# A folded MLP's third pair of up tiles, its copies and squares, its low parts and its even turns put in another order

## The reference, cut to what matters

```
def mlp_sq_relu(hn, w_up, w_down):
    return jnp.square(jax.nn.relu(hn @ w_up)) @ w_down

h = h + mlp_sq_relu(rmsnorm(h, norm_mlp[i]), w_up[i], w_down[i])    # w_up 1024 x 4096, w_down 4096 x 1024
```

## Time and profile before

| what | us |
|---|---|
| median of 3 runs | 2661.4 (2658.84 to 2661.52) |
| profiled execution | 2656.41 |
| its span, first to last instruction | 2654.7 |
| PE matmuls busy | 2531.4 (95% of the span) |
| DVE busy | 1892.3 (71%) |
| ACT busy | 1143.5 (43%) |
| POOL busy | 802.0 (30%) |
| mean granted TensorE clock | 0.989 of full speed |

### The profile page before, as it was taken

One profiled execution on the slowest core, in us unless ns is written; L12 is line 12 of the kernel. 1 busy time (PEld: TensorE's weight loads), 2 busy tenths in 40 slices (PEclk: granted clock), 3 DMA queues, 4 the chain that ended last, 5 costly groups with the idle time before them and its releaser, 6 DMA issues.

```text
span 2654.7 us, 32483 instructions
## 1 busy us (share of the span) xinstructions
PE 2531.4 (95%) x11896; PEld 2081.2 (78%) x11896; DVE 1892.3 (71%) x2552; ACT 1143.5 (43%) x1860; POOL 802.0 (30%) x594
## 2 busy tenths in 40 slices
PE   7999999899999989998999999989999998999898
PEld 6788888787888768886778888878788876788677
DVE  7677655658666789998665657665766678999866
ACT  6555433535434444443442323353534344443344
POOL 2000000034232466664420000002423245666542
PEclk9999999999999999999999999999999999999999
DMA  3000100123333323321221001012233342323122
GB/s 134 29 25 25 32 25 24 56 71 107 104 118 120 123 96 116 107 96 56 88 95 40 25 32 40 24 47 97 80 115 108 115 133 104 109 95 124 52 64 80
DMA packets 78639, 207.63 MB, mean 78 GB/s; under 512 B 8672, under 2 KB 10736, under 8 KB 78496
## 3 DMA queue, kind: packets, MB, share of 16 engines
q1 hardware_dynamic: 75552, 195.85, 22.3%
q0 software_dynamic: 2224, 7.54, 0.8%
q10 hardware_dynamic: 720, 2.36, 0.2%
HBM read 163.25 MB, written 42.47 MB: 77 GB/s over the span
## 4 chain that ended last, share of the span: by engine, by line
PE 57%; issue 18%; DVE 15%; ACT 4%; POOL 3%; DMA 2%; DVEq 0%; ACTq 0%; POOLq 0%; SPq 0%
PE gemm_ps L732 8%; PE gemm_ps L734 8%; PE gemm_ps L733 8%; PE s_ps L732 7%; PE s_ps L733 6%; PE s_ps L734 6%; DVE wlo L2303 3%; PE to_ps L733 3%; PE to_ps L734 3%; PE to_ps L732 3%; DVE a_blocks L2390 2%; DMA hid_raw<-hidden 2%; DVE b_blocks_lo L2390 2%; POOL hid_raw L1244 2%; PE to_ps L838 1%
## 5 line engine op out<-in xcount | busy, mean ns | idle before, releaser
L732 PE MATMUL gemm_ps<-a_hi,whi 128*128 128x512 f32 x1024 | 424.4, 414 | 20.7 <-DVE a_lo L1914 10.7
L734 PE MATMUL gemm_ps<-a_hi,wlo 128*128 128x512 f32 x1024 | 402.5, 393 | 0.0
L733 PE MATMUL gemm_ps<-a_lo,whi 128*128 128x512 f32 x1024 | 401.5, 392 | 0.0
L732 PEld LDWEIGHTS gemm_ps<-a_hi,whi 128*128 128x128 f32 x1024 | 194.3, 190 | 61.1 <-issue 20.4
L2303 DVE TENSOR_TENSOR wlo<-wraw,whi 128x512 fp32r<-128x512 f32 (+1 forms) x204 | 213.9, 1049 | 33.3 <-ACT whi L1595 32.8
L1244 POOL TENSOR_TENSOR hid_raw<-hid_raw 128x512 f32<-128x512 f32 x120 | 197.0, 1650 | 103.2 <-DVE a_blocks L2390 42.3
L734 PEld LDWEIGHTS gemm_ps<-a_hi,wlo 128*128 128x128 f32 x1024 | 193.3, 189 | 42.8
L733 PEld LDWEIGHTS gemm_ps<-a_lo,whi 128*128 128x128 f32 x1024 | 194.4, 190 | 32.6 <-issue 1.4
L732 PE MATMUL s_ps<-a_blocks,whi 128*128 128x512 f32 x448 | 179.5, 401 | 31.4 <-DVE zt L2356 15.1
L2303 DVE TENSOR_TENSOR wlo<-wraw_a,whi 128x512 fp32r<-128x512 f32 (+1 forms) x204 | 175.6, 861 | 34.7 <-ACT whi L1595 33.7
L1595 ACT ACTIVATE whi<-wraw_a 128x512 fp32r<-128x512 f32 (+1 forms) x204 | 122.5, 602 | 168.5 <-PE s_ps L734 131.8
(11 more groups left out here) (392 smaller groups left out, 6347.0 us busy)
## 6 DMA issues: line engine op xcount, KB each, us to landing
wraw<-panels SPq DMA_DIRECT2D x90, 512.0 KB, 3.6
wraw<-folds SPq DMA_DIRECT2D x60, 512.0 KB, 4.3
wraw_a<-folds SPq DMA_DIRECT2D x60, 512.0 KB, 4.4
hid_raw<-hidden SPq DMA_DIRECT2D x120, 256.0 KB, 4.0
hidden<-sumsq SPq DMA_DIRECT2D x64, 256.0 KB, 3.5
hidden<-zs SPq DMA_DIRECT2D x32, 256.0 KB, 2.1
hidden<-zt SPq DMA_DIRECT2D x32, 256.0 KB, 2.0
h<-x_t SPq DMA_DIRECT2D x11, 512.0 KB, 5.4
```

The source lines that it names most:

```text
L732: nc.tensor.matmul(out, hi_w, hi_x, start=start, stop=False, skip_group_check=True)
L733: nc.tensor.matmul(out, hi_w, lo_x, start=False, stop=False, skip_group_check=True)
L734: return nc.tensor.matmul(out, lo_w, hi_x, start=False, stop=stop, skip_group_check=True)
```

## The change

- **Third pair sooner.** `RAMP` takes tile 2's parts in from (16, 3) to (17, 2) instead of (16, 5) to (17, 4). SP issues all four loads of tile 2 before the last stores of turn 15, and the loads of tile 3 before the raw weights of turn 19.
- **Copies ahead of squares.** In turn 16 ACT's squares of turn 15 move from blocks 0 and 1 to blocks 1 and 2, behind the copy of bank A.
- **Low parts.** `t3_lo` is gone; DVE makes block 4's low parts at (0, 0), and its others in turn 0 move to later blocks. The weights' low part at (0, 4) is made after the read of bank E.
- **Even turns.** At (n, 0) of turns 20, 22 up to 32, DVE's `w_ahead` moves behind `out_of(n, 0)`. GpSimd's S1 and S3 move from blocks 0 and 2 to blocks 2 and 4 in turns 20, 22 up to 30.

```diff
 RAMP = {...
-        (15, 6): [(0, 6), (1, 2)], (16, 0): [(1, 3)], (16, 1): [(1, 4)], (16, 2): [(1, 5)], (16, 3): [(1, 6)],
-        (16, 5): [(2, 0)], (16, 6): [(2, 1)], (17, 0): [(2, 2)], (17, 1): [(2, 3)],
-        (17, 2): [(2, 4)], (17, 3): [(2, 5)], (17, 4): [(2, 6)]}
+        (15, 6): [(0, 6), (1, 2)], (16, 0): [(1, 3)], (16, 1): [(1, 4)], (16, 2): [(1, 5)],
+        (16, 3): [(1, 6), (2, 0)], (16, 4): [(2, 1)], (16, 5): [(2, 2)], (16, 6): [(2, 3)],
+        (17, 0): [(2, 4)], (17, 1): [(2, 5)], (17, 2): [(2, 6)]}
+
+DEFERRED = [(0, 4)] + [(n, 0) for n in range(UPS + 4, TURNS, 2)]
...
-UP_LO = [x for x in UP_ORDER if x[0] != 4]
+UP_LO = UP_ORDER
...
                     elif n == 1:
-                        sp.wait_ge(up_t3_ready, 4 * layer + 3)
+                        sp.wait_ge(up_lo_ready, len(UP_LO) * layer + UP_LO.index((4, 2)) + 1)
...
                     store(n, B_RAW["B11"], C11, 1, c11_stored)
                     if n == UPS - 1:
-                        load_hidden(2, "B11")
+                        for name in ("B11", "B12", "B22", "B21"):
+                            load_hidden(2, name)
                     store(n, B_RAW["B22"], C22, 2, c22_stored)
-                load_hidden(2, "B12")
-                load_hidden(2, "B22")
                 store(UPS - 1, B_RAW["B12"], C12[(UPS - 1) % 2], 3, c12_stored[(UPS - 1) % 2])
-                load_hidden(2, "B21")
                 store(UPS - 1, B_RAW["B21"], C21, 4, c21_stored)
                 for n in range(UPS, TURNS):
                     s = n - UPS + 2
-                    if n + 2 < TURNS:
+                    if s != 3 and n + 2 < TURNS:
                         load_raw(n + 2)
                     if 2 < s < SUBS:
                         for name in ("B11", "B12", "B22", "B21"):
                             load_hidden(s, name)
+                    if s == 3:
+                        load_raw(n + 2)
...
-                def t3_lo(kk):
-                    gp.wait_ge(up_hi_ready, len(UP_ORDER) * layer + UP_ORDER.index((4, kk)) + 1)
-                    hi, lo = up_block(4, kk)
-                    nc.gpsimd.tensor_tensor(lo, late_part("T3", kk), hi, ALU.subtract).then_inc(up_t3_ready, 1)
...
-                for kk in range(4):
-                    t3_lo(kk)
                 for n in range(TURNS):
                     for j in range(BLOCKS):
                         if n == LAST - 2 and j == 0:
                             tail_adds(0)
-                        if n < LAST and j == 0:
+
+                        later = n >= UPS + 4 and n % 2 == 0 and n < LAST - 1
+                        if n < LAST and j == (2 if later else 0):
                             w_sum(n + 1, "S1")
-                        if n < LAST and j == 2:
+                        if n < LAST and j == (4 if later else 2):
                             w_sum(n + 1, "S3")
...
-                        if 1 <= n <= UPS and j == 0:
+                        if 1 <= n <= UPS and j == n // UPS:
                             square(n - 1, 2)
                             square(n - 1, 3)
-                        if 1 <= n <= UPS and j == 1:
+                        if 1 <= n <= UPS and j == 1 + n // UPS:
                             square(n - 1, 4)
...
                             if j == 1:
                                 t_part("T4", 3)
-                            for x in {1: late[0:2], 2: late[2:5], 3: late[5:8]}.get(j, ()):
+                            for x in late[0:4] if j == 0 else late[2 * j + 2:2 * j + 4]:
                                 up_lo(*x)
                         if j:
                             out_of(n, j - 1)
                         elif n:
                             out_of(n - 1, BLOCKS - 1)
+                        if (n, j - 1) in DEFERRED:
+                            w_ahead(n, j - 1)
                         for s, i in taken_in(n, j):
                             hid_lo(s, i)
-                        w_ahead(n, j)
+                        if (n, j) not in DEFERRED:
+                            w_ahead(n, j)
```

More of the change, by code:

```diff
@@ L443, in build_trunk @@
         up_g_ready, up_t_ready, up_hi_ready = sem("up_g_ready"), sem("up_t_ready"), sem("up_hi_ready")
-        up_lo_ready, up_t3_ready = sem("up_lo_ready"), sem("up_t3_ready")
+        up_lo_ready = sem("up_lo_ready")
         c22_ready, relu_ready, hid_ready = sem("c22_ready"), sem("relu_ready"), sem("hid_ready")
@@ L673, in load_hidden @@
                         sp.wait_ge(up_lo_ready, len(UP_LO) * (layer + 1))
-                        sp.wait_ge(up_t3_ready, 4 * (layer + 1))
                     elif s == 1:
@@ L980, in input_block @@
                     if n < UPS:
-                        if n == 0 and j == 4:
-                            pe.wait_ge(up_t3_ready, 4 * layer + i + 1)
-                        elif n == 0:
+                        if n == 0:
                             pe.wait_ge(up_lo_ready, len(UP_LO) * layer + UP_LO.index((j, i)) + 1)
```

## The result

| | before | after |
|---|---|---|
| median | 2661.5 us (4 runs, 2658.8 to 2662.2) | 2634.1 us (4 runs, 2630.5 to 2636.1) |
| profiled execution | 2656.4 | 2636.1 |
| its span | 2654.7 | 2634.5 |

The ratio is 0.9904, 95% interval 0.989 to 0.9919: 1% faster, which is clear of the scatter. The forecast was 2632.6 us, range 2618 to 2646.

What follows compares the result with a forecast made beforehand. PE stands still or runs slowly some 40 us a layer, nearly always waiting for DVE, held up by POOL. Gains 11.6 + 4.8 + 0 + 12.2 + 0.2 = 28.8 us off 2656.4 give 2627.6, median 2632.6 us, range 2618 to 2646.

Steps and rivals of the forecast that it cites:

- Third pair: Turns 16 to 18: tile 2 and tile 3's load sooner, 12.2 us gained in both layers (bounds 6 and 17).
- Copies ahead of squares: Turn 16: the copy gains 0.4 us at block 2 and block 3 gives it back; worth 0.
- Even turns: Turns 20 to 31: PE's stall for DVE's read of bank A goes, 11.6 us gained (bounds 8 and 12.4).
- signs named beforehand: What the changed profile would show in turns 0, 18, 20 to 31 and 32: waits, turn lengths, a fallen clock.
- the deferred low part costs nothing: Even turns, turn 22: block 3's weights end by 1030.5 us, and PE wants them at 1032.4.
- moving S1 and S3 costs nothing visible: Even turns: the S's come some 6 us later, and their first user is block 1 of the next turn.
- Turn 32: Turn 32: low part behind the bank A read, still held through POOL's six operations; 4.8 us gained (bounds 4 and 16).
- The rival that POOL lets DVE in: Turn 32: DVE waits for one POOL operation, not six; 11 us better, 2621.4 us (chance 0.22).
- the 1.2 us at the start of turn 18: Third pair: DVE's pauses shrink in turns 16 and 17, winning 1.2 us (0 to 2).
- Low parts of block 4: Turn 0: block 6 starts 0.9 us sooner, layer 0 loses its clock; 0.2 us gained in sum.
- the 1.6 us for the clock in layer 0: Turn 0: PE idles 3.5 us at block 6, so layer 0 loses its full clock too, costing 1.6 us.
- The other rivals: Third pair gains nothing, 2644.8 us (chance 0.15); nothing is won, 2661 (0.03); third pair's parts hold up weights, 2679 (0.04).

Runs made afterwards that it cites:

- the late transfer: The changed kernel with GpSimd's transfer p_raw<-p_t issued behind its adds of the third turn from the end; 2626.1 us (one run).

## Why the prediction was right, and where its terms were off

The sign was right for the reasons given: each of the four parts gave its gain alone, and by the mechanism named but for the 1.2 us of the third pair. That the time was right to 1.5 us is in part luck. Two terms were too large by 7.1 us together and two too small by 4.2, which gives 28.8 us forecast and 25.9 measured in the turns. That the medians lie 27.3 apart is also scatter in unchanged code. Of the signs named beforehand two were missed in size only: turns 20 to 31 took 230.3 to 230.7 us, not 228.5 to 229.5, and turn 18 took 21.1, not 20.5.

- **Even turns**: mechanism right, no wait for bank A is left, and the part alone gives 4.6 and 4.4 us. The size was off, 8.4 against 11.6, near the lower bound of 8. The step that was off is that the deferred low part costs nothing because PE wants the weights only at 1032.4. I looked at who needs the deferred operation and not at what stands behind it: the input's low part, 1.78 us beside POOL (991.15). The order could not be turned either, as that part is ready late. And "moving S1 and S3 costs nothing visible" was true but missed what the move is worth: without it DVE's order brings 1.6 us of the 4.6.
- **Turn 32**: I took the end at which POOL holds DVE off to the end of its six operations, and the trace shows it: 5.09 us, PE waiting at block 3 for 3.07 us. Turn 32 gave 3.05 and 2.86 us for 2.4, and turn 33 another 0.55 and 0.76, which I had not counted. The rival that POOL lets DVE in fell; the late transfer showed that another 3.8 us a layer were to be had in turn 32 (of which layer 1 gave about 1 back in turn 33, where the clock fell).
- **Copies ahead of squares**: nothing, confirmed by putting them back.
- **Third pair**: the wait for a transfer at (18, 0) is gone, and turn 18 took 21.09 and 21.13 us where I had 20.5. The term that failed is the 1.2 us at the start of turn 18. I had the 1.3 us pause of DVE for tile 2's T1 stay (it is 1.31 again), and turns 16 and 17 took 31.99 us together for 31.83 before, so nothing was won there. I had left out ACT, which sat 5.55 us in front of the same T1 with a copy behind it. That explains the new stall at block 6 and not the missing 1.2 us: with the stall cured the three turns were no shorter. What bounds them is DVE's work, as I had said: four orders of these parts took 52.9 to 53.5 us, of which DVE was busy 49.8 to 50.9.
- **Low parts of block 4**: PE idled 3.3 us at block 6 as forecast (3.5; these lengths are counted from when the next matmul was due, where the timeline's idle shows 3.10 for this one and 2.63 for the 2.8 of before), and turn 0 is 1.0 us shorter at full clock (0.9 forecast). What failed is the 1.6 us for the clock in layer 0. The clock did fall there, and in layer 1, where it had fallen before, it did not. Over all profiles of this study, turn 0 ran with a fallen clock in 5 of 10 cases with an idle stretch of 2.8 us at block 6, in 7 of 14 with 3.3 us, and in none of 4 with 2.1 us. I had taken one trace's pattern, one layer in two, for a property of the length. A fall is worth some 1.5 us (2.4 once), and it came in half of the cases at either length, so in these 24 cases the step from 2.8 to 3.3 us showed no cost. Nor does the length alone decide: behind the 3.2 us at block 3 of turn 32 (3.07 in the timeline) the clock fell in 9 of 10 cases.
- **The other rivals** fell: the third pair gained 8.3 us, turns 20 to 31 won 8.4, and the kernel was not slower.

## What to carry to other kernels

When an operation is put off in a full queue, ask what it now stands in front of, and whether that work was ready: here the put-off part fitted into a pause of 1.1 us, and the one other place tried for it lost nearly all of the gain. A stall that is cured on an engine whose queue is full comes back some blocks later; DVE's busy share in the very turn (15.31 of 15.34 us) tells so before the edit is made. And where GpSimd issues a transfer and then computes without a pause, look at what VectorE does beside it: moving the transfer took 3.8 us off a single turn in each layer.

## What the runs showed of the hardware that was not expected

- A VectorE operation with two SBUF operands, 0.4 us alone, took 5.09 to 6.25 us beside GpSimd's operations where a transfer issued by GpSimd stood ahead of them with no pause; 1.10 and 1.51 us where the transfer came later, one operation of GpSimd each; 0.41 us in a pause of 0.67 us behind the transfer.
- The clock of TensorE fell to its lower level (1.2 of 2.4 GHz) in half of 24 turns 0, after an idle stretch of 2.8 or 3.3 us, with the same stretch in the cases where it held. In turn 32 it fell in 9 of 10 cases after 3.2 us, and the tenth, in the same profile as one of the nine, was 1.6 us shorter. The Trainium skill (TensorE: Matmul & The Clock Gate, HAM oscillation) says that an idle wait for data can throttle TensorE. The runs agree, with 12 falls in the 24 turns 0. Unchanged code scattered by such falls too: most of the 5.6 us between the two profiled executions goes with them.
